# Hybrid DeltaNet and sliding-window trunk on one core: weight remainders at fixed places on VectorE, the q job by quarters first, first visits held over the slot boundary

## What is computed

```python
h = jnp.einsum('btd,dc->btc', x, w_in)          # qa, ka, va, za, ba, aa, qb, kb, vb, zb
ya = _deltanet_group(qa, ka, va, za, ba, aa, conv_w, a_log, dt_bias, norm_w)   # 4 heads of 128, chunked
yb = _swa_group(qb, kb, vb, zb, sinks)          # window 128, 8 query heads on 2 kv heads
y = jnp.einsum('btc,cd->btd', jnp.concatenate([ya, yb], axis=-1), w_out)
return _layernorm(DEEPNORM_ALPHA * x + y, ln_g, ln_b)
```

## Time and profile before

| | us |
|---|---|
| median of 3 runs | 1141.06 |
| lowest and highest | 1137.06, 1141.7 |
| the execution with the profile | 1140.28 |
| its span, first to last instruction | 1137.7 |
| granted clock of TensorE, mean | 0.998 |

### The profile page before, as it was taken

How to read it: one execution, slowest core, us unless ns; L and a number is a source line. 1 busy time by engine, 2 the same in 40 slices (tenths; PEclk the granted TensorE clock), 3 DMA queues, 4 the chain that set the end, 5 groups by cost and what they waited for, 6 DMA issues and landing times. The chain is left out here.

```text
span 1137.7 us, 18323 instructions
## 1 busy us (share of the span) xinstructions
PE 1086.6 (96%) x6700; PEld 864.6 (76%) x6700; DVE 727.6 (64%) x2123; ACT 491.1 (43%) x1427; POOL 88.7 (8%) x116
## 2 busy tenths in 40 slices
PE   6989989899999999999999999999999999999997
PEld 4867767677878888786887878777787878787785
DVE  5466767677474857657466483866637585857564
ACT  3454646473534344263262534336234545363310
POOL 4300000023300000002000000002000000001240
PEclk9999999999999999999999999999999999999999
DMA  7855575645661724352544362625245343522332
GB/s 261 287 208 192 196 240 183 238 144 185 216 224 50 274 86 174 134 166 86 173 148 162 122 241 84 206 80 199 93 167 187 109 162 121 191 81 66 130 103 82
DMA packets 58120, 183.47 MB, mean 161 GB/s; under 512 B 8432, under 2 KB 21168, under 8 KB 44720
## 3 DMA queue, kind: packets, MB, share of 16 engines
q1 hardware_dynamic: 51376, 173.40, 43.9%
q10 hardware_dynamic: 6656, 8.91, 2.7%
HBM read 138.22 MB, written 44.07 MB: 160 GB/s over the span
## 5 line engine op out<-in xcount | busy, mean ns | idle before, releaser
L782 PE MATMUL bank<-xr,w 128*128 128x512 f32 x2496 | 652.1, 404 | 3.2 <-DVE w L1584 2.1
L782 PEld LDWEIGHTS bank<-xr,w 128*128 128x128 f32 x2496 | 450.4, 189 | 102.3 <-issue 14.4
L833 PE MATMUL bank<-wo,y_split 128*128 128x512 f32 x432 | 114.4, 405 | 0.0
L833 PEld LDWEIGHTS bank<-wo,y_split 128*128 128x128 f32 x432 | 77.4, 188 | 16.1 <-issue 1.0
L1254 ACT ACTIVATE score<-score,neg_max 128x256 f32<-128x256 f32 (+1 forms) x128 | 62.8, 492 | 42.1 <-DVE neg_max L1650 42.1
L1466 DVE SCALAR_TENSOR_TENSOR kq<-conv_in,convw_all,kq 128x512 f32<-128x512 f32 x96 | 73.5, 766 | 2.9
L1802 DVE TENSOR_SCALAR t<-bank,nb_rk 128x128 f32<-128x128 f32 x64 | 22.5, 351 | 73.2 <-PE bank L1034 73.2
L1385 ACT ACTIVATE o_scaled<-bank 128x128 f32<-128x128 f32 x64 | 17.6, 275 | 111.3 <-PE bank L1038 111.1
L1805 DVE SCALAR_TENSOR_TENSOR state<-state,cols_all,bank 128x128 f32<-128x128 f32 x64 | 22.2, 346 | 65.9 <-PE bank L1037 65.7
L1109 ACT ACTIVATE conv_in<-bank 128x512 f32<-128x512 f32 x48 | 28.5, 594 | 75.1 <-PE bank L782 73.3
L1684 DVE TENSOR_TENSOR y_step<-blocks,y_cols 128x60 f32<-128x60 f32 (+14 forms) x240 | 47.9, 200 | 14.1 <-DMA blocks<-n_spill 5.1
(11 more groups left out here) (218 smaller groups left out, 1616.1 us busy)
## 6 DMA issues: line engine op xcount, KB each, us to landing
w<-w_split SPq DMA_DIRECT2D x78, 1024.0 KB, 5.0
w_split<-w SPq DMA_DIRECT2D x26, 1024.0 KB, 4.9
blocks<-n_spill ACTq DMA_DIRECT2D x32, 256.0 KB
y_spill<-y_out SPq DMA_DIRECT2D x30, 256.0 KB, 4.2
y_tile<-w_in SPq DMA_DIRECT2D x13, 512.0 KB, 5.9
x_tile<-w_in SPq DMA_DIRECT2D x13, 512.0 KB, 5.8
y_tile<-y_spill SPq DMA_DIRECT2D x12, 512.0 KB, 6.2
x_tile<-x SPq DMA_DIRECT2D x12, 512.0 KB, 3.8
```

What stands on the lines that cost most here:

```text
L782: ins = nc.tensor.matmul(bank[JOBS[at].bank][:], w[:, turn % 3, wp, k, :], xr[:, xp, k], start=(step == 0), stop=(step == 3 * KT - 1))
L833: ins = nc.tensor.matmul(bank[JOBS[at].bank][:], y_place(t)[:, yp, k], wo[:, k, wp, half * UNIT:(half + 1) * UNIT], start=(step == 0), sto ...
```

## The change

- The list of the prologue begins q, ba instead of ba, q; SP's loads begin with x quarter 0, raw tile 0, the other quarters, raw tile 1, then w_ba; the q job waits for the quarters of x one after the other; DVE makes the remainder of turn 0 itself.
- `w_by_pool`: GpSimd makes the remainders of the turns 1 to 8, DVE those of 0 and of 9 to 25.
- DVE's remainders have fixed places (`weight_rest`): after bq ahead of `base_inverses`, after q behind it and `split_y`, ahead of `gate_b`; k's behind the second `convs(n, 0.34, 1)`, ahead of L1782; v's as before; bz's behind the second chunk; z's at the end of the slot.
- A held rounding is now done after the first job of the next slot has been copied, and the last one of the prologue is held too.
- PE: no filling between the key products and the turned queries (`AT_KK`); scores and turned values after 23 matmuls in slots that are neither short nor the last of unit 0; the first turned softmax weights at 0.265 in long slots.
- SP: `load_y(t)` at the start of the slot (in the first slot of a unit, after the spill); ACT: no `after_jobs(n, 0.4)` ahead of `round_y(t)`.

```diff
-        return ["ba", "q", "k", "bT", "v", "kb", "gs", "bz", "gT", "vb", "bq"]
+        return ["q", "ba", "k", "bT", "v", "kb", "gs", "bz", "gT", "vb", "bq"]
...
+def w_by_pool(turn):
+
+    return 0 < turn < 9
...
-AT_KK = 0.04
-AT_SCORES0, AT_VTOK, AT_TURNS0 = 0.09, 0.15, 0.25
...
+        self.scores0, self.vtok = (0.09, 0.15) if short or n == AH - 1 else (23 / fill, 23 / fill)
+        self.turns0 = 0.265 if long else 0.25
...
             load_x(0, 0)
+            load_raw(0)
+            for k2 in range(1, 4):
+                load_x(0, k2)
+            load_raw(1)
             sp.dma_start(ba_raw[:], w_ba).then_inc(ba_in, 16)
-            load_x(0, 1)
-            load_raw(0)
-            load_x(0, 2)
-            load_x(0, 3)
-            load_raw(1)
...
+                if t is not None and 0 < i < AH - 1:
+                    load_y(t)
                 if i < AH - 1:
                     after(sp, pt_ready, n, 2)
...
                     spill_a(n - 1)
+                if t is not None and i == 0:
+                    load_y(t)
...
                 if t is not None and i < AH - 1:
-                    load_y(t)
                     load_x_tile(t)
...
+                if at == 0 and step % 6 == 0:
+                    x_split(pe, 0, step // 6)
...
-                fill_to(n, AT_KK)
                 after(pe, o_scaled_ready, n - 1, 2)
...
-                fill_to(n, AT_SCORES0)
+                fill_to(n, at.scores0)
                 scores(n, 0)
-                fill_to(n, AT_VTOK)
+                fill_to(n, at.vtok)
...
                 if at in W_AT and W_AT[at] + 3 < TILES_W:
-                    if at + 1 < len(JOBS) and JOBS[at + 1].n > max(job.n, -1) >= 0:
+                    split_weight()
+                    if JOBS[at + 1].n > job.n:
                         held.append(W_AT[at] + 3)
...
                 load_blocks(n)
-                split_weight()
                 after_jobs(n, 0.18)
...
-                after_jobs(n, 0.4)
                 if t is not None and i < AH - 1:
                     round_y(t)
...
+            def weight_rest(n, kind):
+
+                turn = W_AT[JOB_AT[kind, n if kind == "z" else n + 1]] + 3
+                if turn < TILES_W and not w_by_pool(turn):
+                    w_low(turn)
...
                 convs(n, 0.2)
+                if n < AH:
+                    weight_rest(n - 1, "bq")
                 after_jobs(n, at.base)
-                w_lows(n, 0.3)
                 if n == SLOTS - 1:
                     split_y(9)
                 base_inverses(n)
                 if t is not None and i < AH - 1:
                     split_y(t)
+                if n < AH - 1:
+                    weight_rest(n, "q")
                 gate_b(n, 0)
...
                 convs(n, 0.34, 1)
-                w_lows(n, at.p16)
                 after(dve, inv_done, n, 2)
...
                 convs(n, 0.34, 1)
+                if n < AH - 1:
+                    weight_rest(n, "k")
                 after(dve, inv_done, n, 4)
...
-                w_lows(n, at.p32)
+                if n < AH - 1:
+                    weight_rest(n, "v")
...
-                    w_lows(n, at.chunk(c, 0.67))
+                    if c == 1 and n < AH - 1:
+                        weight_rest(n, "bz")
...
                 after_jobs(n, 1)
-                w_lows(n, 1)
+                if n < AH - 1:
+                    weight_rest(n, "z")
```

More of the change, by code:

```diff
@@ L40 @@
 TILES_W = 26
-W_POOL = 7
 POOL_TILES = range(8, 12)
@@ L736, in w_low @@
                 pool.wait_ge(w_high, turn + 1)
+                pool.wait_ge(w_ready, turn)
                 lows(flat(1), raw_stage[turn % 2], flat(0)).then_inc(w_ready, 1)
-            for turn in range(W_POOL):
-                w_low(turn)
+            for turn in range(TILES_W):
+                if w_by_pool(turn):
+                    w_low(turn)
             x_low(1, 3)
@@ L979, in slot @@
                     ins.then_inc(ot_done.sem, 1)
-                fill_to(n, AT_TURNS0)
+                fill_to(n, at.turns0)
                 turns(n, 0)
@@ L1234, in _ @@
             x_hi(0, 0)
-            x_hi(0, 1)
             w_hi(0)
-            x_hi(0, 2)
-            x_hi(0, 3)
+            for k2 in range(1, 4):
+                x_hi(0, k2)
             w_hi(1)
@@ L1407, in x_low, with w_low @@
                     .then_inc(x_low_dve, 1)
+            def w_low(turn):
+                flat = lambda part: w[:, turn % 3, part].rearrange("p k n -> p (k n)")
+                dve.wait_ge(w_high, turn + 1)
+                if turn > 0:
+                    dve.wait_ge(w_ready, turn)
+                nc.vector.tensor_tensor(flat(1), raw_stage[turn % 2][:], flat(0), ALU.subtract).then_inc(w_ready, 1)
+            def weight_rest(n, kind):
+                turn = W_AT[JOB_AT[kind, n if kind == "z" else n + 1]] + 3
+                if turn < TILES_W and not w_by_pool(turn):
+                    w_low(turn)
             nc.vector.memset(ones[:], 1.0)
@@ L1417, in _ @@
             nc.vector.memset(lower32[:], 0).then_inc(tail_put.sem, 1)
+            x_low(0, 0)
+            w_low(0)
+            for k2 in range(1, 4):
+                x_low(0, k2)
             dve.wait_ge(ba_in, 16)
@@ L1421, in _ @@
             nc.vector.tensor_tensor(ba_w[:, :, 1], ba_raw[:], ba_w[:, :, 0], ALU.subtract).then_inc(setup, 1)
-            for k2 in range(4):
-                x_low(0, k2)
             dve.wait_ge(const_in, 144)
@@ L1572, in after_jobs @@
                 normalise(n, f)
-            w_place = [W_POOL]
-            def w_lows(n, f):
-                while w_place[0] < TILES_W and JOBS[W_JOBS[w_place[0] - 3]].end + 0.05 <= n + f + 1e-6:
-                    turn = w_place[0]
-                    flat = lambda part: w[:, turn % 3, part].rearrange("p k n -> p (k n)")
-                    dve.wait_ge(w_high, turn + 1)
-                    if turn == W_POOL:
-                        dve.wait_ge(w_ready, W_POOL)
-                    nc.vector.tensor_tensor(flat(1), raw_stage[turn % 2][:], flat(0), ALU.subtract).then_inc(w_ready, 1)
-                    w_place[0] += 1
             beta_place = [0]
@@ L1618, in _ @@
             after_jobs(-1, 1)
-            w_lows(-1, 1)
             def gate_a(n):
```

## The result

The changed kernel takes 1151.02 us (median of 4 runs, 1149.53 to 1154.13), beside 1141.11 for the kernel before in the same session: ratio 1.009, interval 1.0069 to 1.0111. It is slower by 0.9%, little but clear of the noise; the forecast was 1140, and 1147 its upper end. The profiled execution took 1152.13 us, its span 1150.2, against 1140.28 and 1137.7 of before: 12.5 us more in the span.

The account below looks back on a forecast made before the run. TensorE was taken as the bound, busy 1086.6 of 1137.7 us, its idle time mostly ended by VectorE. Terms -1.5, -0.3 and +1.2 made -0.6: 1139.7 from 1140.28, stated as 1140, range 1131 to 1147.

Parts of the forecast that it names:

- Part 1: The start: PE begins about 9.7 and runs without a gap, q and ba through by 21.2; -1.5 us.
- the rule by number: At the start, the clock rises after a number of matmuls: 20 slow ones again, gain 0 instead of 1.5.
- Part 2: Slots 0 to 2, with remainders and held rounding reordered: -0.3 us in all.
- (c): Slots 0 to 2: PE waits 2 to 3.5 us at L782 for bz's remainder; in slot 1 L986 comes 0.6 later.
- (d): Slots 0 to 2: k's remainder ahead of transpose L1782 makes a stall of 1.0 at L1008.
- the second wait of L1034: Slots 0 to 2: bz's own follow-up remainder leaves chunk 0, so L1034 waits once, not twice; -1.5 us.
- Rival D: Slots 0 to 2: v's tile lands 8.1, not 5.8, after issue; ACT delays L1003; +5 to +10, chance 0.18.
- Part 3: Slots 3 to 15: lost filling and later scores against the earlier y load; +1.2 us.
- (e): Without filling between L949 and L961, PE waits at L961 for o_scaled of the slot before; +4.2, ends 2 and 6.
- (f): Slots with 192 matmuls: scores after 23 instead of 18 dense matmuls; about 0.4 in five slots, +2.0.
- (g): Y tile loaded at the slot's start: waits in slots 4, 6, 8 and 10 all go; -5.0.
- Rival B: Bz's remainder is done before PE's matmul 73; slots 0 to 2 at some 54 each, -12, 1128; chance 0.1.

Follow-up runs that it names:

- e7: Kernel before with only bz's weight remainder moved behind the base inverses in slots 0 to 2; 1147.92 us.
- e5: Changed kernel with z's remainder back behind chunk 2 in slots 0 to 2; 1147.72 us.
- e9: As e8, with the y load ahead of the next loads and no hold ahead of its rounding on ScalarE; 1132.88 us, ratio 0.9929.
- e6: Changed kernel with the scores, the transposes of v and the first turns at their old places; 1142.63 us.
- e2: The filled wait: changed kernel plus twelve discarded matmuls ahead of the wait for bz's remainder in slots 0 to 2; 1152.39 us, then median 1147.44.
- e1: Changed kernel with bz's remainder back ahead of the base inverses in slots 0 to 2; 1139.0 us.
- e8: Changed kernel with bz's remainder, L961's filling, scores, y load and z's remainder at their old places; 1136.84 us, ratio 0.9979.

## Why the prediction was wrong, point by point

- **Part 1** was right: slot 0 begins at 55.14 and not 56.73, -1.6 for -1.5. PE starts at 9.39 (9.7 forecast) and runs without a gap up to ba.

```profile
9.39 8.32 PE L794 MATMUL bank<-xr,w 128*128 128x512 f32 x24 [9.39 <-DVE w L1423]
17.55 3.87 PE L809 MATMUL bank<-xr,ba_w 128*16 128x512 f32 x16
```

  Some 14 of these matmuls are slow: the 24 last 8.16 from start to the next line's start, and (17.55 - 9.39 - 24 x 0.23) / (0.424 - 0.23) gives 14, where I had put twelve and the rule by number would have had 20. A fixed number is out. But my reading, a rise that follows the unbroken run, is no rule either. The new start has 8 to 14 slow matmuls in its other profiles, with slot 0 beginning at 54.1 to 55.5. And e7, whose start is that of the kernel before, is at the full pace from the ninth matmul, before any unbroken run, where the kernel before had 20 slow ones. That the rise came at 15.0, near the 14.8 forecast, is in part luck.
- **Part 2** is where it failed. The wait of (c) came with the length and at the matmul forecast (3.1 in each slot; 2 to 3.5 was said), (d) came with 0.9 (1.0), the second wait of L1034 went (-1.4 for -1.5), and z's remainder did no harm to the chunk. What the sum left out is the clock: it took the three matmuls behind the wait at 0.7 and L921 at 0.87, their durations at 2.4 GHz. The step that failed is "then three matmuls (0.7) and L921 (0.87): L986 at 144.2, 0.6 later than now". In slot 1 L997 starts 2.9 later in its slot: the three matmuls and L933 take 3.0 and not 1.6, and the wait ends 0.8 later than forecast. The filled wait measures what the clock costs over the slots: 5.4 to 5.6 us in three. Without it slots 0 to 2 are 174.9 to 175.1, 0.5 to 0.7 over before where -0.3 was forecast. Rival D gave a like time for another reason: ACT never held up L1003. Slot 1's wait of 1.01 for conv_in at the start of v's job was not forecast either; it goes when z's remainder is made earlier (e5), though e9, which makes it as early, has 0.7 of it.
- **Part 3**: (e) was 4.2, though its own terms (5.6 in slots 4, 7, 11 and 15, 0.1 to 0.2 in five more, less 1.4) add up to 4.7 to 5.2; the waits are 5.0, and slots 7 and 11 rose by 0.9 each (forecast 1.0). (f) was to cost 0.4 in five slots; slots 5 and 9 rose by 0.7. The step that failed here is that (f) was priced by the row maxima alone. The decay load waits for what follows them and z's load stands behind it: it is issued 1.1 later in slot 6 and 1.8 later in slot 4, and 4.7 us come back at L782 in this profile, 0 to 3.9 in the six others with late scores. Before, it landed 0.4 ahead of its use (slot 6: 11.7 + 10.0 = 21.7; PE comes to that job at 22.1, as 461.77 - 1.62 - 438.05 in the changed kernel shows). (g): "All go" held in slots 6 and 10. In slots 4 and 8 y's load stands behind the spill and is issued at 25.5 and 25.3 (22.4 and 24.2 before), and PE still waits 0.4 and 1.4 for it (1.1 and 0.6 before; with the scores back, in e6, not at all). There the sentence that SP's queue is only shifted by one issue is wrong too: the next pair load goes from 16.4 to 26.0 and 25.8; no wait of PE for it shows. Slots 4, 6 and 8, for which the terms make +0.2, -1.0 and about -0.2, gave +1.9, +0.3 and +1.9.
- 1.0 in slot 12 is a later broadcast of blocks in this execution; other runs of the same slot have 53.0, or 54.3 to 54.7. Its cause stays open, as with e2.

Rival B (remainders out of the way) had no part in it, and the slower side was D, with 0.18, and 0.14 in all for over 1146.8. A rival that a new wait of 3 us lowers the clock was missing, though the earlier trace rows showed both paces.

## What to carry to other kernels

Where a change adds an idle stretch to TensorE, price the matmuls behind it at the lower clock as well: here a wait of 3.1 us cost about 1.8 us more than its length, on average over three. Look for the slack of the loads queued behind a wait that a change makes later: z's load had 0.4 us in the profile of before, and its landing alone varies by 2. Profile a kernel twice before explaining a wait for a transfer: two profiles of one kernel had theirs in different slots. And a step that lengthens a wait ahead of an in-order engine can be undone alone: moving one remainder back gave 8.7 us in slots 0 to 2, where the change had cost 6.0.

## What was not expected of the hardware

- The granted clock fell to 1.2 GHz behind single waits of 1.75 and 1.71 us (e9, slots 1 and 2) and 1.72 (e1, slot 1), and stayed at 2.4 GHz behind 1.74 (e9, slot 0), 1.70 to 1.75 (e8, slots 0 to 2) and 3.1 (e7, slots 1 and 2; e6, slot 2). The length of the wait alone does not decide. The same slot of the same program had 0.94 or 0.97 of the clock, or 0.97 or 1.00, which moved the time by 1.4 to 1.5 us.
- The same 1 MB load, issued 12.8 us into slot 6 in two profiles of one kernel, landed 10.9 and 8.9 us later. What differs between the two executions is not known.
- GpSimd's subtraction of 2.8 us beside DVE's small steps cost DVE 1.9 us.
